# Low parts of the opening panels released earlier, sums of squares split by token tile, output products started a head sooner

## The reference

```python
def modulate(x, g, shift, scale):
    return rms_norm(x, g) * (1 + scale[:, None, :]) + shift[:, None, :]
...
def short_conv_mixer(h, w_in, w_conv, w_out):
    b_gate, c_gate, v = jnp.split(h @ w_in, 3, axis=-1)
    u = c_gate * v
...
    return (b_gate * conv) @ w_out
...
def mla_mixer(h, positions, w_in, q_a_g, kv_a_g, w_qb, w_kvb, q_g, k_g, w_out):
    q_lat, kv_lat, k_rope = jnp.split(h @ w_in, [Q_LORA, Q_LORA + KV_LORA], axis=-1)
...
    q = rms_norm(q, q_g)
    k = rms_norm(k, k_g)
    q = jnp.concatenate([q[..., :QK_NOPE], apply_rope(q[..., QK_NOPE:], cos, sin)], axis=-1)
    k = jnp.concatenate([k[..., :QK_NOPE], apply_rope(k[..., QK_NOPE:], cos, sin)], axis=-1)
...
        s = jnp.einsum("bqhd,bkhd->bhqk", q[:, start:end], k[:, :end]).astype(jnp.float32) * scale
        p = jax.nn.softmax(jnp.where(mask, s, -jnp.inf), axis=-1).astype(v.dtype)
        outs.append(jnp.einsum("bhqk,bkhd->bqhd", p, v[:, :end]))
    return o @ w_out
...
def reference(x, c, ...):
    for i in range(DEPTH):
        mod = c_act @ ada_w[i] + ada_b[i]
        h = modulate(x, tok_norm[i], sh1, sc1)
        y = short_conv_mixer(h, ...) if i % N_MIXERS == 0 else mla_mixer(h, ...)
        x = x + g1[:, None, :] * y
        h = modulate(x, ch_norm[i], sh2, sc2)
        x = x + g2[:, None, :] * peer_mixer(h, peer_q_w[i], peer_subkeys[i], peer_u[i], peer_v[i])
```

## Time and profile before

| | us |
|---|---|
| median of 3 runs | 1952.1 |
| lowest and highest run | 1951.09, 1956.58 |
| profiled execution | 1953.11 |
| its span in the trace | 1951.4 |
| busy: TensorE, VectorE, ScalarE, GpSimd | 1896.1, 1601.3, 1015.8, 290.7 |

### The profile page before, as it was taken

The page is one execution under the profiler, slowest core; times in us unless marked ns, Lnnn a source line. Parts: engine busy times, 40 slices in busy tenths (PEclk is TensorE's granted clock), DMA queues, the critical chain, the costliest instruction groups (busy, mean ns, idle before and its releaser), DMA issues.

```text
span 1951.4 us, 39787 instructions
## 1 busy us (share of the span) xinstructions
PE 1896.1 (97%) x13027; PEld 1659.5 (85%) x13027; DVE 1601.3 (82%) x3091; ACT 1015.8 (52%) x1638; POOL 290.7 (15%) x171
## 2 busy tenths in 40 slices
PE   6989999999999999999999999999999999999998
PEld 6989898888888888887889898988888888888877
DVE  7747999999999999997764489998888888888866
ACT  4344445555555555554555534455555555555543
POOL 3857400000000000000052473000000000000000
PEclk9999999999999999999998999999999999999999
DMA  8954544777777777777732354455555555555554
GB/s 340 361 198 152 170 141 153 225 223 228 217 225 224 222 222 225 227 225 224 237 101 83 109 163 141 142 150 175 182 179 179 181 181 174 183 178 178 182 183 140
DMA packets 104150, 371.75 MB, mean 191 GB/s; under 512 B 11392, under 2 KB 13824, under 8 KB 103680
## 3 DMA queue, kind: packets, MB, share of 16 engines
q1 hardware_dynamic: 96000, 341.26, 55.2%
q0 software_dynamic: 8064, 29.36, 5.1%
HBM read 369.53 MB, written 1.05 MB: 190 GB/s over the span
## 4 chain that ended last, share of the span: by engine, by line
PE 84%; DVE 10%; DVEq 2%; issue 1%; POOL 1%; ACT 1%; DMA 1%; SPq 0%; POOLq 0%
PE bank L546 36%; PE bank L532 18%; PE bank L534 9%; PE bank L437 4%; PE bank L438 4%; PE bank L439 4%; PE bank L560 2%; DVE w_lo L1187 2%; DVE hot_b L1413 1%; POOL w_lo L1144 1%; DVEq L1419 1%; DVE arena L1304 1%; PE bank L780 1%; DVE arena L1206 1%; DVE arena L1271 1%
## 5 line engine op out<-in xcount | busy, mean ns | idle before, releaser
L839 ACT CAST w_hi<-raw 128x1024 fp32r<-128x1024 f32 (+1 forms) x603 | 630.7, 1046 | 292.9 <-DMA raw<-in_v_panels 103.7
L1187 DVE TENSOR_TENSOR w_lo<-raw,w_hi 128x1024 fp32r<-128x1024 f32 x493 | 603.3, 1224 | 135.2 <-PE bank L534 59.3
L532 PE MATMUL bank<-act_two,w_hi 128*128 128x512 f32 x1536 | 548.1, 397 | 0.0
L534 PE MATMUL bank<-act_two,w_lo 128*128 128x256 f32 x1536 | 430.6, 280 | 0.0
L532 PEld LDWEIGHTS bank<-act_two,w_hi 128*128 128x128 f32 x1536 | 288.5, 188 | 69.0
L546 PE MATMUL bank<-w_hi,wt_hi 128*128 128x512 f32 x1024 | 328.2, 401 | 3.3 <-DVE wt_lo L1452 2.6
L437 PE MATMUL bank<-act_two,w_hi 128*128 128x256 f32 x1060 | 308.2, 291 | 20.1 <-DVE w_lo L1187 12.1
L546 PE MATMUL bank<-w_lo,wt_hi 128*128 128x512 f32 x1024 | 318.9, 393 | 0.0
L546 PE MATMUL bank<-w_hi,wt_lo 128*128 128x512 f32 x1024 | 316.2, 390 | 0.0
L438 PE MATMUL bank<-act_two,w_hi 128*128 128x256 f32 x1060 | 300.7, 284 | 0.0
L439 PE MATMUL bank<-act_two,w_lo 128*128 128x256 f32 x1060 | 300.5, 283 | 0.0
(11 more groups left out here) (226 smaller groups left out, 1956.2 us busy)
## 6 DMA issues: line engine op xcount, KB each, us to landing
raw<-in_u_panels SPq DMA_DIRECT2D x256, 512.0 KB, 3.6
raw<-in_v_panels SPq DMA_DIRECT2D x256, 512.0 KB, 3.6
raw<-in_panels SPq DMA_DIRECT2D x81, 512.0 KB, 4.2
ada<-in_ada_rows POOLq DMA_DIRECT2D x56, 512.0 KB, 4.8
arena<-in_ada_rows SPq DMA_DIRECT2D x40, 512.0 KB, 6.9
raw<-in_panels SPq DMA_DIRECT2D x6, 384.0 KB, 3.2
arena<-in_subkeys SPq DMA_DIRECT2D x2, 1024.0 KB, 6.8
xT<-in_xT SPq DMA_DIRECT2D x1, 1024.0 KB, 6.8
```

Source lines behind the costliest of these rows:

```text
L532: pe.matmul(bank[:, 0:2 * T], w_hi[:, slots[0], w], act_two[:, :, a], start=(k == 0), stop=False, skip_group_check=True)
L534: mm = pe.matmul(bank[:, 0:T], w_lo[:, slots[1], w], act_hi[:, a], start=False, stop=(k == KB - 1), skip_group_check=True)
L839: nc.scalar.copy(w_hi[:, slot, 0:width], raw[:, slot, 0:width]).then_inc(hi_done, 1)
L1187: dve.tensor_tensor(w_lo[:, lo_slot, 0:width], raw[:, slot, 0:width], w_hi[:, slot, 0:width].bitcast(F32), ALU.subtract).then_inc(lo_done, 1)
```

## The change

Four edits, named by the parts of the diff.

1. A new semaphore `pair_lo_used`. `pair_hi` now takes a range of k, and its last piece increments the semaphore behind each panel's last low product. GpSimd's `split_lo` for panels 2 and 3 of the six stages (PAIRS_IN_ORDER) waits for it instead of `pan_done`. GpSimd's loops over conv_out and mla_out are written out.
2. `head_sums` does one tile of 128 tokens at a call. Keys: tile 0, nope panel 0, tile 1, nope panel 1. Queries: tile 0 behind nope panel 3, with waits for the squares two heads at a time and for the third use of the spread scales, then the scores of head 0, then tile 1.
3. mla_out's `pair_hi`: k 0 to 3 at i = HEADS, k 4 and 5 at i = HEADS + 1, k 6 and 7 behind the loop.
4. `rotate` has no work between its two halves; `invert_key_rms` follows it.

```diff
@@ -96,6 +96,7 @@
 
 WIDTHS = {BASE["q_b"] + _j: 2 * Q_LORA for _j in range(6)} | {BASE["k_b"] + _j: 2 * KV_LORA for _j in range(4)}
 MLA_ORDER = (3, 4, 5, 6, 0, 1, 2)
+PAIRS_IN_ORDER = ("conv_in", "conv_out", "sel0", "mla_in", "mla_out", "sel1")
 QB_ORDER = (4, 5, 0, 1, 2, 3)
 TWO_PI = 2.0 * np.pi
 PI_1 = 6.28125
@@ -246,6 +247,7 @@
         hi_done = sem("panel_hi_ready")
         lo_done = sem("panel_lo_ready")
         pan_done = sem("panel_multiplied")
+        pair_lo_used = sem("lo_panel_of_pair_used")
         evac = {n: sem(f"evacuated_{n}") for n, _ in STAGES}
         ada_landed = [sem(f"ada_landed{i}") for i in range(ADA)]
         ada_used = sem("ada_rows_used")
@@ -444,16 +446,18 @@
                 pe.wait_ge(evac[stage], it * unroll + (j + 1))
                 return slots
 
-            def pair_hi(hi, count, slots, acts, half):
+            def pair_hi(hi, count, slots, acts, k0, k1):
 
                 for p in range(2):
                     s = slots[p]
-                    for k in range(half * KB // 2, (half + 1) * KB // 2):
+                    for k in range(k0, k1):
                         if p == 0:
                             pe.wait_ge(hi, count + k + 1)
                         w = slice(k * P, (k + 1) * P)
                         pe.matmul(PAN[p][:, 0:T], w_hi[:, s[0], w], acts[0][k], start=(k == 0), stop=False)
-                        pe.matmul(PAN[p][:, 0:T], w_lo[:, s[1], w], acts[0][k], start=False, stop=False)
+                        mm = pe.matmul(PAN[p][:, 0:T], w_lo[:, s[1], w], acts[0][k], start=False, stop=False)
+                    if k1 == KB:
+                        mm.then_inc(pair_lo_used, 1)
 
             def pair_lo(lo, count, slots, acts):
 
@@ -468,7 +472,7 @@
             def first_pair(hi, lo, count, slots, acts=norm_act):
 
                 for half in range(2):
-                    pair_hi(hi, count, slots, acts, half)
+                    pair_hi(hi, count, slots, acts, half * KB // 2, (half + 1) * KB // 2)
                 pair_lo(lo, count, slots, acts)
 
             def full_panel(stage, j, unroll=0, it=0, acts=norm_act):
@@ -718,16 +722,18 @@
                 for x in range(2):
                     head_panel("q_b", x, TR[x], Q_LORA, QB, norm_act)
 
-                def head_sums(n, nope, rope):
-
-                    for t in range(TT):
-                        o = STAT[:, 16 * n - 8 + 8 * t:16 * n + 8 * t]
-                        for i, (sq_rope, c) in enumerate(rope):
-                            pe.matmul(o, sq_rope[:, t * P:(t + 1) * P], con[:, c:c + HEADS], start=(i == 0), stop=False)
-                        for h in range(HEADS):
-                            mm = pe.matmul(o, nope[:, h * T + t * P:h * T + (t + 1) * P], con[:, C_HEAD + 7 - h:C_HEAD + 15 - h],
-                                           start=False, stop=(h == HEADS - 1))
-                    mm.then_inc(head_sum, 1)
+                def head_sums(n, nope, rope, t, first=0):
+
+                    o = STAT[:, 16 * n - 8 + 8 * t:16 * n + 8 * t]
+                    for i, (sq_rope, c) in enumerate(rope):
+                        pe.matmul(o, sq_rope[:, t * P:(t + 1) * P], con[:, c:c + HEADS], start=(i == 0), stop=False)
+                    for h in range(HEADS):
+                        if first and h % 2 == 0:
+                            pe.wait_ge(head_sq, first + h // 2)
+                        mm = pe.matmul(o, nope[:, h * T + t * P:h * T + (t + 1) * P], con[:, C_HEAD + 7 - h:C_HEAD + 15 - h],
+                                       start=False, stop=(h == HEADS - 1))
+                    if t == TT - 1:
+                        mm.then_inc(head_sum, 1)
 
                 def spread_key_rstd(n):
 
@@ -746,9 +752,12 @@
                     head_panel("q_b", 2 + p, QN[p], Q_LORA, QB, norm_act)
 
                 pe.wait_ge(head_sq, 4)
-                head_sums(1, sqk, [(sqkr[:, x * T:(x + 1) * T], C_FIRST) for x in range(2)])
-                pe.wait_ge(evac["k_b"], 4)
+                key_ropes = [(sqkr[:, x * T:(x + 1) * T], C_FIRST) for x in range(2)]
+                query_ropes = [(sqr[:, (2 * x + i4) * T:(2 * x + i4 + 1) * T], C_GROUP + 4 - 4 * i4)
+                               for x in range(2) for i4 in range(2)]
+                head_sums(1, sqk, key_ropes, 0)
                 nope_panel(0)
+                head_sums(1, sqk, key_ropes, 1)
                 nope_panel(1)
                 pe.wait_ge(key_rstd, 1)
                 for n in range(3):
@@ -760,6 +769,8 @@
                     spread_key_rstd(n)
                 pe.wait_ge(evac["q_b"], 1)
                 nope_panel(3)
+                pe.wait_ge(bc_used, 3)
+                head_sums(2, sqn, query_ropes, 0, 5)
                 out_slots = []
                 for i in range(HEADS + 3):
                     if i < HEADS:
@@ -780,12 +791,12 @@
                                 mm = pe.matmul(o, qz[:, z0:z0 + P], rot[:, k0:k0 + n], start=False, stop=(x == 1))
                         mm.then_inc(s_done, 1)
                     if i == 0:
-                        pe.wait_ge(head_sq, 8)
-                        head_sums(2, sqn, [(sqr[:, (2 * x + i4) * T:(2 * x + i4 + 1) * T], C_GROUP + 4 - 4 * i4)
-                                           for x in range(2) for i4 in range(2)])
+                        head_sums(2, sqn, query_ropes, 1)
+                    if i == HEADS:
+                        out_slots = [wait_panel("mla_out", p) for p in range(2)]
+                        pair_hi(o_hi, 0, out_slots, norm_act, 0, 4)
                     if i == HEADS + 1:
-                        out_slots = [wait_panel("mla_out", p) for p in range(2)]
-                        pair_hi(o_hi, 0, out_slots, norm_act, 0)
+                        pair_hi(o_hi, 0, out_slots, norm_act, 4, 6)
                     if 2 <= i <= HEADS + 1:
                         h = i - 2
                         pe.wait_ge(p_norm, h + 1)
@@ -805,7 +816,7 @@
                         pe.matmul(o[:, P:2 * P], v0, pT[:, h % 2, P:2 * P], start=True, stop=False)
                         pe.matmul(o[:, P:2 * P], v1, pT[:, h % 2, 2 * P:3 * P], start=False, stop=True
                                   ).then_inc(o_done, 1)
-                pair_hi(o_hi, 0, out_slots, norm_act, 1)
+                pair_hi(o_hi, 0, out_slots, norm_act, 6, KB)
                 pair_lo(o_copied, 0, out_slots, norm_act)
                 for j in range(2, 8):
                     full_panel("mla_out", j)
@@ -1140,7 +1151,10 @@
                 slot, lo_slot, _, n = ring(stage, j, unroll, it)
                 width = D if unroll else WIDTHS.get(BASE[stage] + j, D)
                 pool.wait_ge(hi_done, n)
-                pool.wait_ge(pan_done, n + HI - LO)
+                if stage in PAIRS_IN_ORDER and LO <= j < 2 * LO:
+                    pool.wait_ge(pair_lo_used, LO * PAIRS_IN_ORDER.index(stage) + j - LO + 1)
+                else:
+                    pool.wait_ge(pan_done, n + HI - LO)
                 pool.tensor_tensor(w_lo[:, lo_slot, 0:width], raw[:, slot, 0:width],
                                    w_hi[:, slot, 0:width].bitcast(F32), ALU.subtract).then_inc(lo_done, 1)
 
@@ -1156,9 +1170,8 @@
                                rstd[:, T:2 * T].unsqueeze(1).broadcast_to([P, KB, T]), ALU.mult).then_inc(by_rstd, 1)
             for j in range(24):
                 split_lo("conv_in", j)
-            with pool.Fori(0, 2) as it:
-                for j in range(4):
-                    split_lo("conv_out", j, 4, it)
+            for j in range(KB):
+                split_lo("conv_out", j)
             select_panels(0)
             with pool.Fori(0, 96 - ADA_FIRST) as it:
                 pool.wait_ge(ada1_used, it + 1)
@@ -1171,9 +1184,8 @@
             for stage, count in (("v_b", 2), ("k_b", 4), ("q_b", 6)):
                 for j in range(count):
                     split_lo(stage, j)
-            with pool.Fori(0, 2) as it:
-                for j in range(4):
-                    split_lo("mla_out", j, 4, it)
+            for j in range(KB):
+                split_lo("mla_out", j)
             select_panels(1)
 
 
@@ -1546,7 +1558,7 @@
                 select(l)
                 experts(l)
 
-            def rotate(a, b, gains_at, by_cos, to, blocks, between=None):
+            def rotate(a, b, gains_at, by_cos, to, blocks):
 
                 wide = lambda ap: ap.rearrange("p (i t) -> p i t", t=T)
                 cs = cosb.unsqueeze(1).broadcast_to([P, blocks, T])
@@ -1557,8 +1569,6 @@
                     dve.scalar_tensor_tensor(out=wide(by_cos[:, x * n:(x + 1) * n]), in0=wide(half), scalar=g, in1=cs,
                                              op0=ALU.mult, op1=ALU.mult)
                     dve.scalar_tensor_tensor(out=wide(half), in0=wide(half), scalar=g, in1=sn, op0=ALU.mult, op1=ALU.mult)
-                if between is not None:
-                    between()
                 dve.drain()
                 dve.tensor_tensor(to[:, 0:n], by_cos[:, 0:n], b, ALU.subtract)
```

(3 more changed lines are left out.)

## The result

| | before | changed |
|---|---|---|
| median (5 runs each), us | 1954.4 | 1942.8 |
| lowest and highest | 1951.1, 1956.6 | 1940.1, 1945.3 |
| ratio to before | | 0.9941 (0.9930 to 0.9952) |
| profiled execution, span | 1953.1, 1951.4 | 1940.1, 1938.4 |

The change made the kernel 0.6% faster, 11.6 us by the medians. The prediction had 1958.9 us, slower. Rival (a), VectorE keeps the port, had 1942.5. The measured time lies inside the stated range, 1941 to 1963, only because that range was widened to take in the rivals; the forecast's own range was 1953 to 1963.

A forecast was written before the change was run, and what follows sets the result against it. TensorE, busy for 97% of the span, was taken to bound the kernel. From 1953.1 us, stages +3.9, clock falls +6.0, sums −3.0 and pair −1.1 gave 1958.9 us; own range 1953 to 1963, with rivals 1941 to 1963.

The forecast's parts named there:

- Rival (a): GpSimd's split gets the shared port only when VectorE's stream of low activations ends; 1942.5 us, chance 0.20.
- the six waits: TensorE idles before panel 2 in six stages, waiting for GpSimd's low part of the weights; together 8.66 us.
- The port in sel0, mla_in and sel1 (+2.8, +1.9, +2.8): GpSimd's two early splits each hold up VectorE's low activations, so panel 2 starts later by these us.
- conv_in (−0.8): Only the eighth low activation waits for one GpSimd split, so panel 2 still starts 0.8 us sooner.
- conv_out and mla_out (−1.55, −1.25): VectorE reads PSUM and one SBUF tile there, so no stop; the early release gains 1.55 and 1.25 us.
- Falls of the clock behind the holes (+6.0): TensorE's holes in sel0, mla_in and sel1 each bring a fall of the granted clock, costing 2.0 us each.
- Sums of squares (−3.0, bounds 0 and −6.1): In attention, splitting the sums by token tile avoids part of the clock's falls; 3.0 us gained, the middle taken.
- The pair (−1.1): mla_out's ready products fill TensorE's idle 1.63 us before head 6's transposes, so pair_lo comes 1.1 us sooner.
- VectorE's rotation (0): Rotation ahead of the key RMS reorders four short instructions on an engine not last there; 0 us.
- Rival (b): GpSimd takes the port once, its second split coming only behind VectorE's stream; 1947.9 us, chance 0.12.
- port taken twice: The forecast's own case: both GpSimd splits interrupt VectorE's stream in sel0, mla_in and sel1; 1958.9 us, chance 0.55.

The follow-up runs named there:

- sums_whole: The changed kernel with the sums of squares for keys and queries back in one piece; measured twice, 1943.9 and 1943.8 us.
- pause_a: The changed kernel with 4 tiny GpSimd memsets (6 in sel1) before panel 2's split in conv_in, sel0, mla_in and sel1; 1946.7 us.
- pause_b: The changed kernel with 6, 8, 7 and 3 tiny GpSimd memsets before panel 2's split in conv_in, sel0, mla_in and sel1; 1941.2 us.
- release_only: The kernel before with only the early release of the low parts added; 1946.2 us, ratio to before 0.9962.
- no_release: The changed kernel with the early release undone, low parts waiting for pan_done in all six stages; 1951.6 us, ratio to before 0.9991.
- the drained kernel: The changed kernel with a drain behind VectorE's low activations in sel0, mla_in and sel1; 1961.9 us, ratio to before 1.0045.

## Why the prediction was wrong, step by step

- **What bounds the kernel, and the six waits.** Right. Their 8.66 us were what the release could win, and 6.8 of the 9.1 us of such waits went.
- **The port in sel0, mla_in and sel1 (+2.8, +1.9, +2.8).** The step that failed. The sentence "VectorE stops for the whole of GpSimd's instruction, in the middle of a stream too" was drawn from one held addition of 128x48 in a stream of four and carried over to a stream of another operation, of 128x256. There it doesn't hold: no instruction lasted over 0.48 us in the three stages, GpSimd's first split waited for the stream's end instead, and by the lead of one trace over the other the stages gained 0.8, 1.0 and 0.7 us. Rival (a), which named what would decide, had 0.55, 1.0 and 0.55.
- **conv_in (−0.8).** In the changed kernel's trace panel 2 came 0.8 us sooner, and by the mechanism described: one activation late by a split. The same mechanism, right in one stage of four. It isn't sure even there: in sums_whole, pause_a and pause_b the stream stayed whole and panel 2 came 1.7 to 1.8 us sooner than before. The trace before also had the clock low over another stretch of this stage (32.0 to 38.8 us, the changed kernel 37.1 to 40.5), so 0.8 in both is partly luck.
- **conv_out and mla_out (−1.55, −1.25).** Their idle times went from 1.55 and 1.55 to 0 and 0.22. conv_out's lead grew by 3.0 us, not 1.55: in the trace before, the high part of its second panel came late (GpSimd waited 1.50 us for it), in the changed one it did not. release_only shows 1.15 of it and no_release none, so it varies and I don't count it.
- **Falls of the clock behind the holes (+6.0).** No hole, no fall. In the drained kernel, where the holes are, there are falls of 6.8 us in each of the three stages, some 3.4 us of time each, longer than the 3.5 (2.0 us of time) that I took.
- **Sums of squares (−3.0, bounds 0 and −6.1).** Mis-sized. About −1 by the medians, −4.5 in the one pair of traces: within the bounds, too large at the middle. A price taken from one profiled execution was taken from a thing that varies by 17 us of low clock between executions.
- **The pair (−1.1).** The lead at pair_lo grew by 0.9 us (1087.63 to 1076.61, with 10.1 ahead of it), near the forecast; whole-run times don't confirm it.
- **VectorE's rotation (0).** No run takes this edit back alone, so the 0 is not shown.
- **The sum.** With −6.2 for the release instead of +3.9 (0.8 + 1.55 + 0.8 + 1.0 + 1.3 + 0.7, the leads, with conv_out by its idle time) and 0 for the falls, the same sum gives 1953.1 − 6.2 − 3.0 − 1.1 = 1942.8 us, the measured median, partly by luck: the sums gave less, and the release's medians more. Rival (a)'s 1942.5 is as close by the same luck, though its mechanism is the one that the traces show in three stages. Rival (b)'s own terms add up to 1948.3, not 1947.9.

The chance of 0.55 for "port taken twice" was too high for a rule taken from one small instruction and extended to a larger one of another operation, beside 0.20 for the case that came true.

## What to carry to other kernels

Before you price a conflict between two engines from a row, look whether the row's instructions have the operation, the size and the spacing of yours: here a stream without gaps kept the other engine out, and a drain behind each of its instructions turned a gain of 9 us into a loss of 9. Where an operand comes late, ask first whether the consumer can take it last; by the medians that gave as much as handing over its buffer earlier, though less of it was idle time. And where the granted clock varies between executions, read its low time in more than one trace before you put a price on it.

## What was not expected of the hardware

- A GpSimd instruction that waits for the shared port is on record as running: 3.79 us for a split of 2.40.
- VectorE's back-to-back instructions of 128x256 with two SBUF inputs kept GpSimd out for up to 1.4 us and three more instructions, 33 times of 33, though small ones (128x48 and less, of another operation) did not the earlier trace rows; with drains between them GpSimd got the port by the next gap. In conv_in it got in ahead of the last instruction 9 times of 12, all nine at a granted clock of 0.50; why is open.
- The time at the lower clock in one execution of one program was 13.7 us and 30.7 us in another, four falls in the same neighbourhood, three of them longer in the second, and one more.
